# Gate and up products of an expert as two groups, with the scatter of the expert before between them

## The reference, cut to what matters

```python
hg = jnp.einsum('td,edf->tef', t, w_gate[sl])
hu = jnp.einsum('td,edf->tef', t, w_up[sl])
act = jax.nn.silu(hg) * hu * weights[:, sl, None]
out = out + jnp.einsum('tef,efd->td', act, w_down[sl])
```

## Time and profile before

| | |
|---|---|
| median of 3 runs | 1262.27 us (1261.66 to 1262.52) |
| the profiled execution | 1261.49 us, its span 1259.5 us |
| TensorE matmul busy | 967.8 us, 77% of the span |
| weight loads busy | 613.5 us, 49% |
| VectorE, ScalarE busy | 396.3 us, 190.0 us |
| moved by DMA | 436.63 MB, 347 GB/s in the mean |
| mean granted TensorE clock | 0.889 of full speed |

### The profile page before, as it was taken

One profiled execution on the slowest core, in us unless ns is written; L12 is line 12 of the kernel. 1 busy time (PEld: TensorE's weight loads), 2 busy tenths in 40 slices (PEclk: granted clock), 3 DMA queues, 4 the chain that ended last, 5 costly groups with the idle time before them and its releaser, 6 DMA issues.

```text
span 1259.5 us, 26471 instructions
## 1 busy us (share of the span) xinstructions
PE 967.8 (77%) x10996; PEld 613.5 (49%) x10996; DVE 396.3 (31%) x1212; ACT 190.0 (15%) x533; POOL 8.8 (1%) x27
## 2 busy tenths in 40 slices
PE   5999979666678787986689998886666666666964
PEld 5867855333334443543377777543333333333432
DVE  3767453111112222221156674521111111111213
ACT  2345211000001010110113442110000000000001
POOL 2000000000000000000000000000000000000000
PEclk9999979888889998997879999798888888787977
DMA  9925159999999999899993342499999999999994
GB/s 319 364 86 201 68 167 426 426 425 427 427 425 424 426 425 426 369 425 426 405 383 124 114 155 100 191 426 426 427 425 427 426 426 427 426 425 425 425 427 173
DMA packets 45962, 436.63 MB, mean 347 GB/s; under 512 B 8064, under 2 KB 10112, under 8 KB 21248
## 3 DMA queue, kind: packets, MB, share of 16 engines
q1 hardware_dynamic: 45824, 434.72, 83.5%
HBM read 433.65 MB, written 1.05 MB: 345 GB/s over the span
## 4 chain that ended last, share of the span: by engine, by line
PE 46%; DMA 40%; DVE 6%; issue 5%; DVEq 2%; ACT 1%; SPq 1%; ACTq 0%
DMA ring<-in_w_up 39%; PE ps L557 16%; PE ps L623 7%; PE ps L568 4%; PE ps L746 4%; PE ps L635 2%; PE ps L538 2%; PE ps L577 2%; PE ps L686 1%; PE ps L708 1%; SPq L442 1%; PE ps L629 1%; PE ps L725 1%; PE ps L640 1%; PE ps L693 1%
## 5 line engine op out<-in xcount | busy, mean ns | idle before, releaser
L557 PE MATMUL ps<-ring,xg 128*32 128x256 f32 x4096 | 317.3, 478 | 188.4 <-DMA ring<-in_w_up 187.5
L557 PEld LDWEIGHTS ps<-ring,xg 128*32 128x32 f32 x4096 | 171.2, 136 | 318.7 <-issue 274.9
L1047 DVE SCALAR_TENSOR_TENSOR gu<-th,ps 128x128 f32<-128x128 f32 x72 | 20.7, 287 | 616.1 <-ACT th L854 616.1
L568 PE MATMUL ps<-ring,actT 128*32 128x256 f32 x2304 | 139.2, 382 | 15.2 <-issue 12.8
L568 PEld LDWEIGHTS ps<-ring,actT 128*32 128x32 f32 x2304 | 69.0, 109 | 76.3 <-DVE actT L1051 24.0
L854 ACT ACTIVATE th<-ps 128x128 f32<-128x128 f32 x72 | 20.0, 277 | 528.0 <-PE ps L557 528.0
L623 PE MATMUL ps<-hT,ring 128*128 128x256 f32 x416 | 95.9, 389 | 1.7 <-DVE hT L1097 1.7
L623 PEld LDWEIGHTS ps<-hT,ring 128*128 128x128 f32 x416 | 80.1, 195 | 13.8 <-ACT hT L902 2.3
L577 PE MATMUL ps<-ysb,PwT 32*128 32x256 f32 x1024 | 73.3, 400 | 1.0 <-ACT ysb L858 1.0
L538 PE MATMUL ps<-xh,Pb 128*32 128x256 f32 x1024 | 69.2, 387 | 0.0
L746 PE MATMUL ps<-ring,hT 128*128 128x256 f32 x256 | 60.9, 397 | 2.1 <-ACT hT L970 1.4
(11 more groups left out here) (250 smaller groups left out, 787.8 us busy)
## 6 DMA issues: line engine op xcount, KB each, us to landing
ring<-in_w_gate SPq DMA_DIRECT2D x64, 2048.0 KB, 43.1
ring<-in_w_up SPq DMA_DIRECT2D x64, 2048.0 KB, 37.6
ring<-in_w_down SPq DMA_DIRECT2D x64, 2048.0 KB, 42.1
ring<-in_w_in SPq DMA_DIRECT2D x8, 2048.0 KB, 20.2
ring<-in_w_out SPq DMA_DIRECT2D x4, 2048.0 KB, 19.8
ring<-in_w_in SPq DMA_DIRECT2D x2, 1584.0 KB, 22.9
x<-in_x SPq DMA_DIRECT2D x1, 1024.0 KB, 5.1
out<-fin SPq DMA_DIRECT2D x2, 512.0 KB, 2.7
```

The costliest lines, as they stand in the source:

```text
L557: last = mm(b_gate[j * SLOTS:(j + 1) * SLOTS, 0:2 * GQ], tokens[:, k, :], ring[:, low:high + 1:high - low, o:o + GQ], start=(k == 0), stop ...
L568: last = mm(b_y[j * SLOTS:(j + 1) * SLOTS, 0:DQ], actT[:, c * SLOTS:(c + 1) * SLOTS], ring[:, slot, o:o + DQ], start=(c == 0), stop=(c == ...
```

## The change

`hidden` is split into `gate` and `up`. Each waits for its own chunk, has 64 MATMUL records of 128 moving columns (and 64 weight loads), writes a bank of its own (up: free columns of the bank of y) and has its own semaphore, which frees its own slot. TensorE's order becomes gate(e), combine(e-1), up(e), gather(e+1), down(e), places(e+1). VectorE waits for up only ahead of its second step. `REACH` goes; the planned slots stay the same but for six chunks of layer 1.

```diff
-    return (li, 1 + n, 1 if part == "down" else 0)
+    return (li, 1 + n, ("gate", "up", "down").index(part))
...
-        if part == "up":
-            usable = [f for f in usable if abs(f[1] - slot_of[li, "gate", n]) <= REACH]
...
-                    sp_.wait_ge(M["down_mm" if part == "down" else "hidden_mm"], li * NE + n + 1)
+                    sp_.wait_ge(M[part + "_mm"], li * NE + n + 1)
...
-            def hidden(S, tokens, li, e):
-                (a, a_signal, a_count), (b, b_signal, b_count) = chunk(li, "gate", e), chunk(li, "up", e)
-                low, high = min(a, b), max(a, b)
-                pe.wait_ge(a_signal, a_count)
-                pe.wait_ge(b_signal, b_count)
+            def gate(S, tokens, li, e):
+                slot, signal, count = chunk(li, "gate", e)
+                pe.wait_ge(signal, count)
                 for k in range(KC):
                     for j in range(NQ):
                         o = k * FF + j * GQ
-                        last = mm(b_gate[j * SLOTS:(j + 1) * SLOTS, 0:2 * GQ], tokens[:, k, :],
-                                  ring[:, low:high + 1:high - low, o:o + GQ], start=(k == 0), stop=(k == KC - 1))
-                last.then_inc(S["hidden_mm"], 1)
+                        last = mm(b_gate[j * SLOTS:(j + 1) * SLOTS, 0:GQ], tokens[:, k, :],
+                                  ring[:, slot, o:o + GQ], start=(k == 0), stop=(k == KC - 1))
+                last.then_inc(S["gate_mm"], 1)
+
+            def up(S, tokens, li, e):
+                slot, signal, count = chunk(li, "up", e)
+                pe.wait_ge(signal, count)
+                for k in range(KC):
+                    for j in range(NQ):
+                        o = k * FF + j * GQ
+                        last = mm(b_y[j * SLOTS:(j + 1) * SLOTS, DQ:DQ + GQ], tokens[:, k, :],
+                                  ring[:, slot, o:o + GQ], start=(k == 0), stop=(k == KC - 1))
+                last.then_inc(S["up_mm"], 1)
...
                     pe.wait_ge(M["xg_ready"], n)
-                    hidden(M, xg[e % 2], li, e)
-                    if e + 1 < NE:
-                        pe.wait_ge(M["prep_ready"], 2 * n + 1)
-                        gather(M, Pb[(e + 1) % 2])
+                    gate(M, xg[e % 2], li, e)
                     if e > 0:
                         pe.wait_ge(M["y_copied"], n - 1)
                         pe.wait_ge(M["places_copied"], n - 1)
                         combine(M, PwT[(e - 1) % 2], ysb)
+                    up(M, xg[e % 2], li, e)
+                    if e + 1 < NE:
+                        pe.wait_ge(M["prep_ready"], 2 * n + 1)
+                        gather(M, Pb[(e + 1) % 2])
                     pe.wait_ge(M["actT_ready"], n)
                     down(M, li, e)
...
-                        hidden(V, xgx, li, e)
+                        gate(V, xgx, li, e)
                         if n > 1:
                             pe.wait_ge(M["y_copied"], n - 1)
+                        up(V, xgx, li, e)
...
-                act.wait_ge(S["hidden_mm"], n)
+                act.wait_ge(S["gate_mm"], n)
...
                 dve.drain()
-                v.scalar_tensor_tensor(actv[:, :], gu[:, :], 0.5, b_gate[:, GQ - o:2 * GQ - o], ALU.mult, ALU.mult)
+                dve.wait_ge(S["up_mm"], n)
+                v.scalar_tensor_tensor(actv[:, :], gu[:, :], 0.5, b_y[:, DQ:DQ + GQ], ALU.mult, ALU.mult)
```

More of the change, by code:

```diff
@@ L66 @@
 CHUNK = KC * PW
-RING, LATE, REACH = 8, 2, 7
+RING, LATE = 8, 2
 WEIGHTS = ([("in", n) for n in range(len(W_IN_PIECES))] + [("out", n) for n in range(len(W_OUT_PIECES))]
@@ L367, in build_encoder @@
         landed = [sem(f"landed{i}") for i in range(RING + LATE)]
-        names = ("prep_ready", "gather_mm", "xg_ready", "places_mm", "places_copied", "hidden_mm", "tanh_ready", "actT_ready",
+        names = ("prep_ready", "gather_mm", "xg_ready", "places_mm", "places_copied", "gate_mm", "up_mm", "tanh_ready", "actT_ready",
                  "down_mm", "y_copied", "combined")
@@ L384, in chunk @@
             return slot, landed[slot], 16 * USES[li, part, n]
-        def gate_half(li, e):
-            return int(chunk(li, "gate", e)[0] > chunk(li, "up", e)[0]) * GQ
         def passes_before(eng, e):
@@ L851, in act_tanh @@
             def act_tanh(S, li, e, n):
-                act.wait_ge(S["hidden_mm"], n)
-                o = gate_half(li, e)
-                A(th[:, :], b_gate[:, o:o + GQ], ACT.Tanh, scale=0.5).then_inc(S["tanh_ready"], 1)
+                act.wait_ge(S["gate_mm"], n)
+                A(th[:, :], b_gate[:, 0:GQ], ACT.Tanh, scale=0.5).then_inc(S["tanh_ready"], 1)
             def y_copy(S, y, n):
@@ L1045, in activate @@
                 dve.wait_ge(S["tanh_ready"], n)
-                o = gate_half(li, e)
-                v.scalar_tensor_tensor(gu[:, :], th[:, :], 1.0, b_gate[:, o:o + GQ], ALU.add, ALU.mult)
+                v.scalar_tensor_tensor(gu[:, :], th[:, :], 1.0, b_gate[:, 0:GQ], ALU.add, ALU.mult)
                 dve.drain()
-                v.scalar_tensor_tensor(actv[:, :], gu[:, :], 0.5, b_gate[:, GQ - o:2 * GQ - o], ALU.mult, ALU.mult)
+                dve.wait_ge(S["up_mm"], n)
+                v.scalar_tensor_tensor(actv[:, :], gu[:, :], 0.5, b_y[:, DQ:DQ + GQ], ALU.mult, ALU.mult)
                 dve.drain()
```

## The result

The changed kernel takes 1274.15 us (median of 4 runs, 1269.52 to 1275.41) beside 1261.97 us before: ratio 1.0083, 95% interval 1.006 to 1.0105 (a ratio in this document is not the quotient of the two medians, which would be 1.0097 here). It is slower; the forecast was 1258.2 us, faster. The profiled run took 1269.52 us (span 1267.8 us), 8 us above the one of before. The other three took 4 to 6 us more than it, and no profile shows why.

What follows compares the result with a forecast made beforehand. The weight stream was taken as the bound, except where it stops, with TensorE the bound late in layer 0's experts. Terms 0.8 - 2.3 + 0.3 - 1.65 + 1.3 - 2.5 = -4.05 us from 1262.27 gave 1258.2 us; range 1251 to 1282.

Steps and rivals of the forecast that it cites:

- Late code: Rival: the four other entries into extra-pass blocks in layer 0's stretch also wait for instructions, +22 us, 1280 us; chance 0.10.
- Part 1: Main experts in layer 0's stretch where TensorE is the bound: +0.82 us an expert, +6.6 us for eight.
- Part 2: Extra passes in layer 0's TensorE-bound stretch: -0.28 us a pass, -2.0 us for seven.
- Part 3: End of layer 0's TensorE-bound stretch: gate's slot comes free after 2.14 us, not 3.66 us, so -1.5 us.
- Part 4: Entry into layer 0's TensorE-bound stretch, expert 13: gate is multiplied while up lands, so down starts 2.3 us earlier.
- Parts 5 and 7: Ends of layers 0 and 1: down waits only for its own chunk, -2.3 us (-2.8 before clock loss) and -2.5 us.
- Part 6: Start of layer 1: gate of expert 0 takes 3.6 us in place of 5.3, so the weight stream starts 1.65 us earlier.
- Part 8: Traffic of 9216 added instructions: +1.3 us in layer 1 and +0.3 us behind the stop in layer 0.
- Part 9: SyncE's loads, VectorE's new wait for up, ScalarE's copies and the six moved slots: all at nothing.
- a step of 36 ns: Rival: records with 128 columns follow each other more slowly than forecast, +11.9 us, 1270 us; chance 0.22.
- full pace: Rival: records with 128 columns step at 26.7 ns, the pace of the stream, giving 1253.2 us; chance 0.14.
- The serial rival: Rival: weight loads can't run beside the stream, step 53 ns, +46 us, 1304 us; chance 0.06.

Runs made afterwards that it cites:

- after_few: Changed kernel with each group at 32 records of 256 columns in place of 64 of 128, half the instructions: 1262.65 us, ratio 0.9998.
- split_only: Kernel before with only the product cut in two groups of 64 records with 128 columns; order, waits, signal and releases kept: 1286.54 us, ratio 1.0197.

## Why the prediction was wrong

The step that failed is in parts 1 to 4: the working lets TensorE have its instructions whenever it wants them, in the one stretch where TensorE is the bound, although a group now has twice as many. Late code stood at nothing in the sum and only in a rival, to which I had given 0.10. All by the two profiled runs, from the start of down of expert 13 to the load behind the stop: 166.0 us before (351.06 to 517.03), 181.7 us after (348.90 to 530.60), +15.7 us.

- **Part 1.** Expected +0.82 us an expert, measured 8.06 - 7.76 = +0.30 us. The pace cost nothing (26.7 ns, not 30). Gate and up together last 1.89 + 1.77 = 3.66 us to the next group's start in place of 3.48, +0.18 us for a second group. From gather to down it is 1.09 us in place of 0.97, so the uncovered end of the activation cost 0.12 us and not 0.31. The row of one moving column was the wrong neighbour to take: its loads step by 30 ns, and here a whole pair of load and matmul takes less. Why that row is slower is open.
- **Part 2.** Expected -0.28 us a pass, measured 424.99 - 420.33 = 4.66 us against 5.27: -0.61 us.
- **Part 3.** Expected -1.5 us, measured -1.7 us. Parts 1 to 3 so come to 2.4 - 4.3 - 1.7 = -3.6 us, not +3.1.
- **Part 4.** Expected -2.3 us, measured 351.06 - 348.90 = -2.2 us.
- **What stood in their place.** The entries cost 23.1 us in place of 16.4 (+6.7: the second block missed). Waits inside experts are 8.0 us in place of none. By the starts of the groups these stops cost some 1.9 us more than that, in the main since idle time is counted from the end of the last record (0.27 us long), while the next would have started 0.03 us after it. From the start of its gather to the next group outside the pass, an undisturbed pass takes 10.4 us (11.0 before). The three passes behind the long entries take 7.0 us more than that, and the same three passes before took 4.1 us more: +2.8 us, 2.3 of them behind the second entry (granted clock 0.65 from 395 to 405 us; in the same pass before, from 389 to 398 us, 1.00). Together 6.7 + 8.0 + 1.9 + 2.8 - 3.6 = +15.8 us, against 15.7 measured. The rival had the four other entries as its place; one of them missed, and the larger part came inside experts, which its sum did not have. I had seen the 388 instructions in place of 260, and did not ask how fast the queue delivers them: in the kernel before, one expert in 7.76 us is 34 instructions a microsecond and no row shows it to go faster under full traffic; the change wants 48.
- **Parts 5 and 7.** The 2.7 and 2.6 us came; the 0.5 us allowed for the clock in part 5 were 1.8 us in one of the two ends, none in the other.
- **Part 6.** From the first product to the release of gate's slot 818.63 - 815.00 = 3.63 us: -1.7 us, right.
- **Part 8.** Expected 1.3 us in layer 1; from the first load of its experts to the last up product it is 429.3 us in place of 426.6, +2.7 us. Without extra passes the same stretch is 1.7 us longer with 388 instructions an expert than with 260. The traffic was counted a little high: 72 bytes an instruction, where it is 64, so 0.59 MB and 1.4 us at 426 GB/s in all, not 0.66 MB and 1.6 us. Why more than the bytes is paid is not shown.
- **Part 9.** Nothing of it showed.
- **From the stop to the end.** The load behind the stop is 13.6 us late, the end of the profiled execution 8.3 us. Part 5 gave back 0.9 us, part 6 1.7, part 7 2.6, and part 8 took 2.7. Another 2.6 us came from the mixer of layer 1, which is the same in both kernels and ran at a higher clock this time (0.93 from 650 to 683 us, against 0.89 from 637 to 672 us before; then 1.00 against 0.66 for some 5 us). No run shows that the change has a part in this; take it for luck of the one execution.
- **The range.** The measured 1274 us lie inside 1251 to 1282 us. That is luck: the upper part of the range stood for a step of 36 ns and for missed entries, and the largest piece of the loss, stops inside experts, was in neither sum. The rival "full pace" had the step right (26.7 ns), and its 1253.2 us were off by 21 us, as it had no late code either.
- **The serial rival.** The step of 26.7 ns at 128 columns leaves nothing for loads in series. The rule of the Trainium skill (page "TensorE: Matmul & The Clock Gate", section "Part 3: Packing small matmuls — row/col tiling"), that loads overlap only where the row group differs, does not hold for this kernel's column tiles. The same section also lets a load for the background weight buffer run ahead of matmuls in flight, which the rule as I used it leaves out; whether that is what happens here no trace tells.

## What to carry to other kernels

Splitting a product to start its parts earlier doubles its instructions, and these have to be delivered too: where an engine is the bound and the DMA engines are full, count instructions per microsecond against the fastest stretch that the trace shows under the same traffic, and look for instruction packets that land just ahead of where the engine goes on. Look for the places where the split can pay (here the first and the last expert of a layer) and leave the rest as it is. A stretch in which the stream stops because an engine is behind turns each microsecond of that engine into one of the kernel, so it has to be priced apart from all others.

## What the hardware showed that I had not expected

- Pairs of a 32-column weight load and a 128-column float32 matmul record, four column tiles side by side, run at 26.7 ns each, about half of the 52 ns with 256 columns.
- TensorE ran dry of instructions in straight code at some 48 instructions a microsecond beside 426 GB/s of weights (8.0 us over eight experts), and hardly at all at 34 (0.8 us in after_few), or beside a quarter of the bytes for each chunk (1.1 us in a layer). In the changed kernel and in split_only it went on 1.2 to 1.5 us behind the landing of a 16 KB packet of 256 instructions.
- Entering a block of code far off costs 5.7 to 7.9 us under full traffic where it costs at all, and still up to 6.5 us with a quarter of the bytes. In layer 0 the last 3 us of it lie behind the landing of an instruction packet, whatever the traffic. How many entries of the same six pay this went from two to three to five from kernel to kernel, and did not follow the size of the blocks.
